# The v phase of a two-block network in wide groups, six of its turns as seven block products

## The chip, the cores and the metric

The kernel runs on one core of a Trainium2 chip. Its time is the device time of one execution in microseconds; lower is better. The time before is the median of three executions.

## The reference

Two blocks run one after the other on x of 256 tokens by 2048 features, all in float32. What touches the change is the first projection of the first block:

```python
h = rmsnorm(x, a_norm)                     # (256, 2048)
z = h @ a_w_in                             # (2048, 3 * 4096): [u | v | gate]
u, v, gate = jnp.split(z, 3, axis=-1)
u = jax.nn.gelu(u)
v = rmsnorm(jax.nn.gelu(v), v_gain)        # over all 4096 columns
sv = einsum('gpq,bnqgc->bnpgc', w_s, v in 8 groups of 512 columns) + b_s
x = x + (u * sv * silu(gate)) @ a_w_out
```

The second block (attention, an mLSTM, a feed-forward layer of 5632 with a convolution) follows. Its last product, `(silu(u_gate) * u_val) @ w_down`, is the "down" phase below.

## The kernel before

**Precision.** Each float32 product is made of three: both operands are split into a high part, the value rounded to the matmul's input type, and a low part, the rest. TensorE adds high by high, high by low and low by high. A matmul has 128 rows of depth, 128 tokens (t = 0 or 1) and 512 columns.

**Chunks and the ring.** Weights come from HBM as a stream of chunks of 256 rows by 512 columns, two blocks of depth side by side (128 x 1024 elements, 512 KB). Four slots hold a chunk and its two parts. SP issues the load when the low part of the chunk four before is made (`load_chunk`, L357). ScalarE makes the high part (`high_of_chunk`, L764) when the load has landed and TensorE is done with the chunk four before; VectorE makes the low part (`low_of_chunk`, L1090); TensorE then multiplies: 12 matmuls per chunk in the v phase (`tokens`, L409), for two blocks of depth, two token tiles and three parts. Each engine runs its own queue in the order in which the code issues it: in the loop of a phase, step n issues `split`, the part of chunk n + 4, and after it whatever else the engine has to do at that step.

**The v phase** is the first: 64 chunks, eight groups of eight. A group gives 512 columns of v for both token tiles in one pair of PSUM banks (`G[0]` or `G[1]`). After a group ScalarE reads the banks with Gelu into `v_all` (`v_out`, L820, its instructions have L779), which also sets the banks free (`group_read`). After the last group the sum of squares of v is taken over all 4096 columns in one piece per token tile, tile 0 on ScalarE (L846) and tile 1 on VectorE (L1192). x itself arrives in five loads; ScalarE and VectorE split it (`in_high`, `in_low`) between the first chunks. The norm's scale for x comes from squares of a second copy, `x_first`, on ScalarE (L834). Before the first operand is there, TensorE runs products of a tile of ones (L457), `WARM_UP` of them.

**The down phase** is the last. It works in wide groups: 1024 output columns, so that four chunks (two rows of chunks by two column halves) form a 2 x 2 block matrix of 256 x 512 blocks, one "turn". A turn of the plain kind is those four chunks (C0, C1 of half 0, C2, C3 of half 1), 48 matmuls. In three turns per group the 2 x 2 block product is made with seven products instead (Strassen's scheme in Winograd's form), of six matmuls each. Each of the seven takes one block, or a sum of blocks, of the weights (128 x 1024 elements again, and again split into high and low), and one block, or a sum, of the activations. The sums of weight blocks are made in place by VectorE (`block_sums`, L1094), four per turn. The sums of activations are made once (`sums_of_rows`, L1541 to L1547) and then split. Products 2, 4 and 3 add straight into banks of the result; 1, 5, 6 and 7 gather in four banks of their own (`XS`), which VectorE combines at the end of a group (`add_products`). A turn by products is mixed with a plain turn's four chunks: the order of its 11 items is `MIXED = (1, "C0", 5, 7, "C1", 6, 3, "C2", 4, 2, "C3")`. `blocks` hold the four weight blocks; SP loads them ahead of items 1, 7 and 4, when the last use of the same block in the turn before is over, in one queue with the chunks.

## Time and profile before

| | us |
|---|---|
| median of three executions | 2125.35 |
| lowest, highest | 2124.49, 2126.13 |
| profiled execution | 2127.12 |
| its span, first to last instruction | 2125.3 |
| TensorE busy | 2116.2 |
| VectorE busy | 1313.1 |
| ScalarE busy | 1045.8 |

The profile records one execution. Matmuls overlap (one that is shown with 390 ns starts 227 ns after the one before), so TensorE's busy share says that it always had something under way, not that it ran at its peak. PE stands for TensorE's matmuls, PEld for its weight loads, DVE for VectorE, ACT for ScalarE, SP for SyncE, which here only issues loads.

### The profile page before, as it was taken

The numbers are of one execution on the slowest core, as the hardware profiler recorded it, in microseconds if no ns is written. First come the engines' busy times: TensorE is split into PE (matmuls) and PEld (weight loads), VectorE is DVE, ScalarE is ACT, GpSimd is POOL, SyncE is SP. The second block draws the span as 40 slices with busy tenths as digits, with TensorE's granted clock in tenths as the row PEclk, the third lists the DMA queues.
The fourth block names the chain that finished last, engine by engine and source line by source line (L and its number), as shares of the span: only waits on it lengthen the run. The fifth ranks groups of instructions, "written<-read, shape, count | busy, mean of one in ns | idle before, by whom it ended". The sixth has DMA issues, their size and how long they took to land.

```text
span 2125.3 us, 24874 instructions
## 1 busy us (share of the span) xinstructions
PE 2116.2 (100%) x10090; PEld 1771.0 (83%) x10090; DVE 1313.1 (62%) x1466; ACT 1045.8 (49%) x1220; POOL 16.6 (1%) x17
## 2 busy tenths in 40 slices
PE   9999999999999999999999999999999999999999
PEld 7888888888888887888888888888888888887887
DVE  5445566656555554554654555567777777779984
ACT  6445444444444444554454444455555555555552
POOL 0000000000000000100000000000000000000000
PEclk9999999999999999999999999999999999999999
DMA  8665566555755555544455565556556556554554
GB/s 303 197 195 172 189 203 204 191 193 179 253 188 188 188 197 170 177 150 149 149 187 190 187 196 186 185 176 189 188 182 195 192 183 194 182 189 178 219 219 157
DMA packets 111810, 404.37 MB, mean 190 GB/s; under 512 B 12496, under 2 KB 13264, under 8 KB 111312
## 3 DMA queue, kind: packets, MB, share of 16 engines
q1 hardware_dynamic: 109440, 394.66, 56.3%
q10 hardware_dynamic: 2256, 8.14, 1.0%
q8 instruction: 79, 1.29, 0.3%
q14 instruction: 35, 0.29, 0.0%
HBM read 400.65 MB, written 2.10 MB: 189 GB/s over the span
## 4 chain that ended last, share of the span: by engine, by line
PE 94%; DVE 4%; DMA 1%; ACT 1%; issue 0%; SPq 0%; ACTq 0%; DVEq 0%
PE g L409 61%; PE xs L428 8%; PE g L428 8%; PE g L693 5%; PE xs L432 4%; PE g L432 4%; DVE w_lo L1090 2%; PE xs L452 1%; DMA raw<-in_stream 1%; PE xs L714 1%; DVE block L1094 1%; PE xs L573 1%; PE g L714 1%; PE xs L481 1%; ACT w_hi L764 0%
## 5 line engine op out<-in xcount | busy, mean ns | idle before, releaser
L1090 DVE TENSOR_TENSOR w_lo<-raw,w_hi 128x1024 fp32r<-128x1024 f32 x719 | 877.5, 1224 | 758.7 <-ACT w_hi L764 755.2
L764 ACT ACTIVATE w_hi<-raw 128x1024 fp32r<-128x1024 f32 x719 | 760.9, 1059 | 956.2 <-PE g L409 643.5
L409 PE MATMUL g<-w_hi,in_both 128*128 128x512 f32 x1536 | 478.5, 391 | 3.3 <-DVE w_lo L1160 3.3
L409 PE MATMUL g<-w_hi,mid_both 128*128 128x512 f32 x1280 | 406.5, 393 | 0.0
L409 PEld LDWEIGHTS g<-w_hi,in_both 128*128 128x128 f32 x1536 | 289.7, 189 | 63.7 <-DVE in_both L1153 3.5
L409 PE MATMUL g<-w_lo,in_both 128*128 128x512 f32 x768 | 299.8, 390 | 0.0
L409 PEld LDWEIGHTS g<-w_hi,mid_both 128*128 128x128 f32 x1280 | 240.4, 188 | 49.6
L409 PE MATMUL g<-w_lo,mid_both 128*128 128x512 f32 x640 | 249.2, 389 | 0.0
L428 PE MATMUL g<-mlp_both,w_hi 128*128 128x512 f32 x704 | 176.7, 393 | 0.4 <-DVE xw L1449 0.4
L428 PE MATMUL xs<-mlp_both,w_hi 128*128 128x512 f32 x704 | 176.3, 392 | 0.0
L409 PEld LDWEIGHTS g<-w_lo,in_both 128*128 128x128 f32 x768 | 144.9, 189 | 29.7
L428 PEld LDWEIGHTS g<-mlp_both,w_hi 128*128 128x128 f32 x704 | 126.6, 189 | 23.5 <-DVE xw L1449 0.8
L428 PEld LDWEIGHTS xs<-mlp_both,w_hi 128*128 128x128 f32 x704 | 126.6, 189 | 22.6
L409 PEld LDWEIGHTS g<-w_lo,mid_both 128*128 128x128 f32 x640 | 120.3, 188 | 23.9
L432 PEld LDWEIGHTS xs<-mlp_both,w_lo 128*128 128x128 f32 x704 | 96.0, 190 | 6.9
L432 PEld LDWEIGHTS g<-mlp_both,w_lo 128*128 128x128 f32 x704 | 96.0, 190 | 6.9
L409 PE MATMUL g<-w_hi,y_hi 128*128 128x512 f32 x256 | 100.0, 390 | 0.0
L693 PE MATMUL g<-w_hi,f_hi 128*128 128x512 f32 x256 | 99.8, 390 | 0.1
L409 PE MATMUL g<-w_hi,y_lo 128*128 128x512 f32 x256 | 99.6, 389 | 0.0
L693 PE MATMUL g<-w_lo,f_hi 128*128 128x512 f32 x256 | 99.6, 389 | 0.0
L693 PE MATMUL g<-w_hi,f_lo 128*128 128x512 f32 x256 | 99.6, 389 | 0.0
L409 PE MATMUL g<-w_lo,y_hi 128*128 128x512 f32 x256 | 99.6, 389 | 0.0
(263 smaller groups left out, 2049.8 us busy)
## 6 DMA issues: line engine op xcount, KB each, us to landing
raw<-in_stream SPq DMA_DIRECT2D x719, 512.0 KB, 3.5
block<-in_stream SPq DMA_DIRECT2D x24, 512.0 KB, 5.4
x_first<-in_x_tokens ACTq DMA_DIRECT2D x1, 2048.0 KB, 9.8
gain_row<-in_gain_rows SPq DMA_DIRECT2D x8, 256.0 KB, 2.7
xt<-in_x_tokens ACTq DMA_DIRECT2D x1, 2048.0 KB, 8.3
xf<-in_x SPq DMA_DIRECT2D x3, 512.0 KB, 9.3
out<-xw ACTq DMA_DIRECT2D x3, 512.0 KB, 3.1
final_row<-in_final_rows ACTq DMA_DIRECT2D x1, 1024.0 KB, 13.3
```

The lines of the kernel that those rows point to most:

```text
L409: ins = mm(G[buf][:, t, :], a[:, kt, at_t], w[:, slot, j * COLS:(j + 1) * COLS], start=(kt == 0 and n == 0), stop=(last and j == ROWS_PER_ ...
L428: mm(UP[buf][:, b, :, :], w_hi[:, slot, j * COLS + b * P:j * COLS + (b + 1) * P], a_both[:, :, kt, :], start=(kt == 0), stop=False, skip_g ...
L432: ins = mm(UP[buf][:, b, 0, :], w_lo[:, slot, j * COLS + b * P:j * COLS + (b + 1) * P], a_both[:, 0, kt, :], start=False, stop=(last and j ...
L452: ins = turn(TR[:, b, t * P:(t + 1) * P], of[:, t, b * P:(b + 1) * P], ident[:])
L481: ins = mm(SV[:, t, :], w[:, t, :], a[:, t, :], start=(n == 0), stop=(n == 2))
L573: ins = mm(to, q[:, t * P:(t + 1) * P], k[:, 0:w], start=n >= HEADS, stop=True, skip_group_check=True)
L693: ins = mm(GG[:, bank, :], a[:, kt, t * P:(t + 1) * P], w[:, slot, half_chunk(j)], start=opens(g, bank), stop=(row == 21 and j == 1 and a ...
L714: ins = mm(bank, a, w[:, slot, half_chunk(j)], start=opens(g, name), stop=(name < 0 and s == BY_PRODUCTS - 1 and j == 1 and n == 2), skip_ ...
L764: activation(w_hi[:, n % RING, :], of[:], ACT.Copy).then_inc(hi_ready, 1)
L1090: v.tensor_tensor(w_lo[:, n % RING, :], of, w_hi[:, n % RING, :].bitcast(F32), ALU.subtract).then_inc(lo_ready, 1)
L1094: v.tensor_tensor(blocks[to][:], blocks[a][:], blocks[b][:], ALU.subtract).then_inc(sem["block_sums"], 1)
```

## The change

The code that described the down phase alone (`DOWN`, `SUMS_AT`, `BY_PRODUCTS`) becomes a list `ITEMS` over all phases, and the v phase is put into wide groups too: four groups of 1024 columns, each with four turns. In `WIDE_STEPS` a pair (a, None) is a plain turn a; (a, b) is plain turn a mixed with turn b by products. The v phase thus has 82 items (19, 22, 19, 22 by group) in place of 64 chunks: items 0 to 7 are plain, 8 to 18 the first mixed turn. The last step of a v group that is mixed has an order of its own, `MIXED_END`, in which half 0 of the result is done at product 2.

```diff
-WARM_UP = 11
+WARM_UP = 17
+WIDE_STEPS = {
+    "v": (((0, None), (1, None), (2, 3)),
+          ((0, 2), (1, 3)),
+          ((0, None), (1, 3), (2, None)),
+          ((0, 2), (1, 3))),
+    "down": (((3, None), (4, None), (8, None), (9, None), (5, 0), (6, 1), (7, 2), (10, None)),
+             ((3, 0), (4, 1), (5, 2), (6, None), (7, None), (8, None), (9, None), (10, None))),
+}
+SUM_TURNS = {"v": (3, 2), "down": (0, 1, 2)}
+SUMS_AT = {"v": (3, 6), "down": (7, 9, 11)}
 MIXED = (1, "C0", 5, 7, "C1", 6, 3, "C2", 4, 2, "C3")
+MIXED_END = (1, "C0", 5, 7, 6, 3, "C1", 4, 2, "C2", "C3")
...
+            def opens(item, bank):
+                key = (item.phase, item.group, bank)
...
+                    _, _, read = group_of(item.phase, 2 * item.group + bank // 2)
+                    if read > 1:
+                        pe.wait_ge(group_read[bank // 2], read - 1)
```

ScalarE at the start splits x later against the chunks, takes the squares of `x_first` at steps 6 and 7 (before 4 and 5), makes the high part of the sums of rows, copies product 1 out of its bank, and applies Gelu in place on what VectorE has written, with the squares of each 512 columns behind it:

```diff
             high_of_chunk(1)
-            in_high(2, 4, 8)
             high_of_chunk(2)
             high_of_chunk(3)
-            in_high(3, 8, 12)
...
+            in_high(2, 4, 8)
+            def sums_high(phase, n):
+                if n in SUMS_AT[phase]:
+                    i = SUMS_AT[phase].index(n)
+                    act.wait_ge(sem["sums_ready"], sums_ahead(phase) + i + 1)
+                    activation(wide[phase].sums_hi[:, i], wide[phase].sums[:], ACT.Copy).then_inc(sem["sums_hi_ready"], 1)
...
+            def v_out(q):
+                act.wait_ge(group_read[q % 2], q // 2 + 1)
+                at_v = v_all[:, :, col_block(q)]
+                by_token(at_v, at_v, ACT.Gelu_apprx_tanh, scale).then_inc(sem["v_ready"], 1)
+                act.wait_ge(sem["v_ready"], q + 1)
+                for t in range(2):
+                    ins = activation(v_junk[:, t, :], at_v[:, t, :], ACT.Square, accum_out=v_ss[:, t, q:q + 1])
+                ins.then_inc(sem["v_sq_ready"], 1)
+                act.wait_ge(sem["v_sq_ready"], q + 1)
+            for n in range(items_of("v")):
+                split("v", n)
+                if n == 0:
+                    in_high(3, 8, 12)
+                if n == 1:
                     in_high(4, 12, 16)
                     act.dma_start(x_first[:], x_tokens).then_inc(sem["x_first_in"], 16)
...
+                sums_high("v", n)
+                if n in (6, 7):
...
+                first_product("v", n)
+                if n == 14:
                     act.wait_ge(sem["scale_ready"], 1)
+                for q in range(7):
+                    if n == half_end("v", q // 2, q % 2) + 1:
+                        v_out(q)
-            activation(y_hi[:, 0:16, :], v_all[:, 0, :], ACT.Square,
-                       accum_out=v_stat[:, 0:1]).then_inc(sem["v_sq_ready"], 1)
```

The eighth output is made at the first step of the next phase. VectorE combines the products and writes the results (after `split`, which holds the low part and the block sum of item n + 4):

```diff
+            def own_products(n):
+                p1, u_a, u_b, u_d = v_wide.p1, v_wide.u_a, v_wide.u_b, v_wide.u_d
+                for g in range(4):
+                    after = n - product_item("v", g, last_by_products("v", g), 6)
+                    if after == 0:
+                        dve.wait_ge(sem["p1_ready"], g + 1)
+                        dve.wait_ge(mm_done, n + 1)
+                        link(v.tensor_tensor(u_a[:], XS[:, 2, :], p1[:], ALU.add))
+                    if after == 1:
+                        link(v.tensor_tensor(u_b[:], XS[:, 3, :], u_a[:], ALU.add))
+                    if after == 2:
+                        link(v.tensor_tensor(u_a[:], XS[:, 1, :], u_a[:], ALU.add))
+                    if after == 3:
+                        link(v.tensor_tensor(u_d[:], XS[:, 1, :], u_b[:], ALU.add))
+                        dve.sem_inc(sem["own_read"], 1)
+            def v_result(q):
+                half = q % 2
+                dve.wait_ge(mm_done, half_end("v", q // 2, half) + 1)
+                to = v_all[:, :, col_block(q)]
+                by_t = ((v_wide.p1, v_wide.u_b), (v_wide.u_a, v_wide.u_d))[half]
+                for t in range(2):
+                    ins = v.tensor_tensor(to[:, t, :], GG[:, 2 * half + t, :], by_t[t][:], ALU.add)
+                ins.then_inc(group_read[half], 1)
+            for n in range(items_of("v")):
+                split("v", n)
+                if n == 0:
+                    in_low(5, 8, 12)
+                if n == 1:
                     in_low(6, 12, 16)
...
+                sums_of_rows("v", n, norm_in.hi, norm_in.lo)
+                sums_low("v", n)
...
+                own_products(n)
+                for q in range(8):
+                    if n == half_end("v", q // 2, q % 2):
+                        v_result(q)
-            link(v.tensor_tensor_reduce(y_lo[:, 0:16, :].rearrange("p a b -> p (a b)"), v_all[:, 1, :],
...
```

`sums_of_rows` makes a set of sums at step n with n + 1 in `SUMS_AT` (steps 2 and 5 of the v phase) by the same five instructions as in the down phase; `sums_low` follows at steps 3 and 6. SP loads chunks and blocks of both wide phases by the rules that the down phase had (`load_chunk`, `load_blocks`). The chunk and product functions of the down phase become `wide_chunk` and `wide_product`, used by both; a chunk or product that opens a bank waits in `opens` until the bank's last result has been read, which in the v phase VectorE's `v_result` reports and no longer Gelu. The down phase keeps its items and their order.

## Rows read from the trace of the kernel before

**Rows 1.** The page, part 1: busy us, share of the span, instructions.

```profile
PE 2116.2 (100%) x10090; PEld 1771.0 (83%) x10090; DVE 1313.1 (62%) x1466; ACT 1045.8 (49%) x1220; POOL 16.6 (1%) x17
```

**Rows 2.** The page, part 4: shares of the chain that ended last, by engine.

```profile
PE 94%; DVE 4%; DMA 1%; ACT 1%; issue 0%; SPq 0%; ACTq 0%; DVEq 0%
```

**Rows 3.** The waits of TensorE: us in total, times, longest.

```profile
PE xs L714 <- DVE w_lo L1090: 0.8, 3, 0.3
```

**Rows 4.** The chain that ended last, down phase: start us, us, what.

```profile
1963.68 1.36 PE xs L714 x6
...
1966.40 2.72 PE g L693 x12
```

**Rows 5.** Stretches: PE, PEld, DVE, ACT, POOL busy (count), PEclk, DMA, GB/s.

```profile
20.00:186.50 166.50, 166.50 (x736) 137.94 (x735) 77.05 (x70) 78.34 (x82) 1.53 (x1) 1.00 0.64 214
...
1952.97:1973.00 20.03, 19.59 (x85) 15.62 (x84) 17.23 (x15) 11.33 (x12) 0.00 (x0) 1.00 0.47 184
```

**Rows 6.** Instructions of VectorE behind the v phase, in order of time.

```profile
188.06 4.42 DVE L1192 CUSTOM_DVE_ANT_0 y_lo<-v_all 128x4096 fp32r<-128x4096 f32 x1
```

**Rows 7.** Instructions of VectorE, down phase: start us, us, engine, line, what.

```profile
1958.03 1.22 DVE L1090 TENSOR_TENSOR w_lo<-block,w_hi 128x1024 fp32r<-128x1024 f32 x1
1959.17 1.22 DVE L1090 TENSOR_TENSOR w_lo<-raw,w_hi 128x1024 fp32r<-128x1024 f32 x1
1960.30 1.22 DVE L1090 TENSOR_TENSOR w_lo<-block,w_hi 128x1024 fp32r<-128x1024 f32 x1
1961.62 1.23 DVE L1094 TENSOR_TENSOR block<-block,block 128x1024 f32<-128x1024 f32 x1
...
1987.77 0.68 DVE L1555 TENSOR_TENSOR u_a<-xs,p 128x512 f32<-128x512 f32 x1
```

**Rows 8.** Instructions of ScalarE, down phase; in brackets the wait before.

```profile
1952.27 1.06 ACT L764 ACTIVATE w_hi<-raw 128x1024 fp32r<-128x1024 f32 x1 [2.95 <-DMA raw<-in_stream]
...
1966.50 1.06 ACT L764 ACTIVATE w_hi<-raw 128x1024 fp32r<-128x1024 f32 x1 [0.30 <-PE g L714]
```

**Rows 9.** Instructions of VectorE that make the sums of rows, down phase.

```profile
1911.56 1.22 DVE L1541 TENSOR_TENSOR f_turn<-f_hi,f_lo 128x1024 f32<-128x1024 f32 x1
1912.82 0.43 DVE L1544 TENSOR_TENSOR f_sums<-f_turn 128x256 f32<-128x256 f32 x1
```

**Rows 10.** Instructions of ScalarE at 29, 186 and 652 us.

```profile
29.29 1.90 ACT L834 ACTIVATE x_junk<-x_first 128x2048 f32<-128x2048 f32 x1
...
186.66 1.25 ACT L779 ACTIVATE v_all<-g,scale 128x512 f32<-128x512 f32 x2
...
652.62 0.61 ACT L792 ACTIVATE sq_junk<-xt 128x512 f32<-128x512 f32 x1
...
653.23 0.62 ACT L792 ACTIVATE sq_junk<-xt 128x512 f32<-128x512 f32 x1
```

**Rows 11.** Instructions of TensorE and ScalarE at the start of the span.

```profile
1.05 4.14 PE L457 MATMUL xs<-ones 128*128 128x128 f32 x22 [1.05 <-DVE ones L1147]
...
8.50 0.77 PE L409 MATMUL g<-w_hi,in_both 128*128 128x512 f32 x1 [3.31 <-DVE w_lo L1160]
...
16.53 1.06 ACT L764 ACTIVATE w_hi<-raw 128x1024 fp32r<-128x1024 f32 x1 [1.14 <-DMA raw<-in_stream]
```

**Rows 12.** A matmul of a product in the down phase, with its wait.

```profile
1959.31 0.50 PE L714 MATMUL xs<-w_hi,sums_hi 128*128 128x512 f32 x1 [0.29 <-DVE w_lo L1090]
```

**Rows 13.** DMA issues, 1930 to 2070 us: count, KB each, median us to landing.

```profile
block<-in_stream SPq DMA_DIRECT2D x20, 512.0 KB, 5.4
```

**Rows 14.** Busy time by stretch at the start, with the granted clock (PEclk).

```profile
4.00:5.00 1.00, 1.00 (x10) 1.00 (x9) 0.00 (x0) 0.00 (x0) 0.00 (x0) 1.00 0.97 315
...
7.00:8.00 1.00, 0.00 (x0) 0.00 (x0) 0.82 (x2) 1.00 (x4) 0.00 (x0) 0.74 1.07 406
...
8.50:14.10 5.60, 5.60 (x13) 4.43 (x14) 5.13 (x10) 5.60 (x12) 0.00 (x0) 0.50 1.02 412
```

**Rows 15.** DMA issues of the first 60 us.

```profile
x_first<-in_x_tokens ACTq DMA_DIRECT2D x1, 2048.0 KB, 9.8
```

More of the change, by code:

```diff
@@ L105 @@
+FIRST_ITEM["end"] = len(ITEMS)
+ITEM_AT = {item: n for n, item in enumerate(ITEMS)}
+CHUNK_ITEMS = [n for n, item in enumerate(ITEMS) if not item.product]
 CHUNK_COUNT = {n: c for c, n in enumerate(CHUNK_ITEMS)}
+QUADS = [(item.phase, item.group, item.turn) for item in ITEMS if item.product == 1]
 B11, B12, B22, B21 = range(4)
@@ new lines, in opens_own, with wide_chunk @@
+            def opens_own(item):
+                key = (item.phase, item.group, -item.product)
+                new = key not in opened
+                if new:
+                    opened.add(key)
+                    if wide_ahead(item.phase, item.group):
+                        pe.wait_ge(sem["own_read"], wide_ahead(item.phase, item.group))
+                return new
+            def wide_chunk(item, a_hi, a_lo, slot):
+                last = ITEM_AT[item] == FIRST_ITEM["end"] - 1
+                order = [(j, t) for j in range(2) for t in range(2)]
+                if last:
+                    order.sort(key=lambda jt: jt[1])
+                for j, t in order:
+                    kt = 2 * item.row + j
+                    if item.phase == "v" and ITEM_AT[item] == 0 and kt == 1 and t == 0:
+                        pe.wait_ge(sem["in_lo_ready"], 2)
+                        pe.wait_ge(lo_ready, 1)
+                    bank = 2 * item.half + t
+                    ended = half_end(item.phase, item.group, item.half) == ITEM_AT[item] and j == 1
+                    for n, (a, w) in enumerate(((a_hi, w_hi), (a_hi, w_lo), (a_lo, w_hi))):
+                        ins = mm(GG[:, bank, :], a[:, kt, t * P:(t + 1) * P], w[:, slot, half_chunk(j)],
+                                 start=n == 0 and opens(item, bank), stop=ended and n == 2, skip_group_check=True)
+                    if last and t == 0 and j == 1:
+                        ins.then_inc(sem["first_tile_done"], 1)
+                return ins
@@ new lines, in wide_product @@
+            def wide_product(item, a_hi, a_lo, slot):
+                p, i = item.product, sum_slot(item.phase, item.turn)
+                sums = wide[item.phase]
+                own = {1: 0, 5: 1, 6: 2, 7: 3}
+                last = item.turn == last_by_products(item.phase, item.group)
+                for j in range(2):
+                    if p in (1, 2, 4):
+                        kt = 4 * item.turn + j + (0 if p == 1 else 2)
+                        t = 1 if p == 4 else 0
+                        hi, lo = a_hi[:, kt, t * P:(t + 1) * P], a_lo[:, kt, t * P:(t + 1) * P]
+                    else:
+                        of = {5: 0, 6: 1, 7: 2, 3: 3}[p]
+                        hi, lo = sums.sums_hi[:, i, of, j, :], sums.sums_lo[:, i, of, j, :]
+                    for n, (a, w) in enumerate(((hi, w_hi), (hi, w_lo), (lo, w_hi))):
+                        first = n == 0 and j == 0
+                        if p in own:
+                            ins = mm(XS[:, own[p], :], a, w[:, slot, half_chunk(j)],
+                                     start=first and opens_own(item), stop=last and j == 1 and n == 2,
+                                     skip_group_check=True)
+                        else:
+                            ins = mm(GG[:, RESULT_OF[p], :], a, w[:, slot, half_chunk(j)],
+                                     start=first and opens(item, RESULT_OF[p]), stop=False, skip_group_check=True)
+                return ins
@@ L747, in high_of_chunk @@
             def high_of_chunk(n):
[L749 to L752 removed]
+                item = ITEMS[n]
+                if item.product:
+                    b, uses = PRODUCT_OF[item.product], quad_of(item)
+                    of = wide[item.phase].blocks[b]
                     if item.product in (1, 3, 2):
@@ L1050, in _ @@
                         gate_tanh(i)
-            for n in range(len(DOWN)):
+            for n in range(items_of("down")):
                 if n == 0:
@@ L1580, in _ @@
[L1580 to L1586 removed]
+                if n + 1 == SUMS_AT["down"][0]:
+                    dve.wait_ge(mm_done, FIRST_ITEM["down"])
+                sums_of_rows("down", n, f_hi, f_lo)
```

466 lines of the change are left out of this document (229 added, 237 removed).

## The prediction, made before the changed kernel was built or run

> **What bounds the kernel now.** I read the page's busy shares first: TensorE is busy over the whole span and its weight loads fill 83% [rows 1]. The chain of waits says the same, 94% on TensorE lines [rows 2], and the wait table has hardly anything for TensorE after the start: 0.8 us in three waits, all in the down phase [rows 3]. So the time is the number of matmuls times their pace, plus the start. The pace stands in the chain of the down phase: 12 matmuls take 2.72 us and 6 take 1.36, 0.2267 each [rows 4]. In the v phase VectorE works 77 of 166 us [rows 5]; it has room there. In the down phase, where blocks are already multiplied by seven products, it works 17.2 of 20.0 us per turn and TensorE loses 0.4 us [rows 5]. That phase is the model for what the change puts into the v phase.
>
> **What it removes.** Six turns go from 48 matmuls to 42: 36 x 0.2267 = 8.2 us off the bound engine. (The Trainium skill, "TensorE: Matmul & The Clock Gate", section "Back-to-back issue gap", gives 512 columns about 216 ns; by it the saving would be 7.8 us. The trace has 227, and that decides.) The one-piece square and sum of v behind the phase (VectorE 4.4 us [rows 6], ScalarE as long beside it) goes away too, worth nothing: TensorE never waited there.
>
> **What it adds.** A turn by products is 11 items in place of 8, and each item takes one high part on ScalarE (1.06 us) and one low part on VectorE (they start 1.13 to 1.14 apart), plus four block sums (1.2) [rows 7, 8]. The v phase has 82 items in place of 64 and 24 block sums; per group come four operations that combine products (0.7) and two results of two operations (1.2 each), priced by the same operation in the down phase [rows 7]; two sets of row sums (1.26 + 4 x 0.4, in all 2.75 with their waits, and 1.2 for their low part, as for any of that size) [rows 9]; and on ScalarE two squares behind each Gelu. A Gelu pair is 1.25 [rows 10]; a square pair, priced by the squares of 512 columns (two start 0.61 apart [rows 10]), 1.3: with the waits of each on the one before, 2.65 for an output that took 1.25. Gelu from SBUF has no row; between 1.2 and 1.3 (the nearest rows) it decides nothing. VectorE then has 82 x 1.14 + 24 x 1.2 + 16 x 0.7 + 8 x 1.2 + 2 x 3.95, and 7 for splitting x: 158 us, for 732 x 0.2267 = 166 us of matmuls. As a mean that fits. But the ring holds four items, so VectorE can't use slack more than four items away, and it needs 2.4 us from the end of an item to the end of the low part in its slot (item end 1966.40, high part 1966.50, about 1.1 to the low part, 1.22) [rows 4, 8]. What decides is each place where products stand close. I went through the queues in the order of the new loops with the durations above; all times below are from the start of the span.
>
> *First products (items 8 to 13), 5.7 us lost.* TensorE starts at 8.65 as before and reaches item 8 at 33.0 and item 11 (product 7) at 38.6. VectorE takes the low part of item 6 at 22.2 (ScalarE splits x until 20.4 and hands over item 6 at 22.2; before, item 4 was at 16.5 [rows 11]), then row sums to 26.1, two low parts and the sums' low part to 29.7, sum, low, sum to 33.2, row sums again to 36.0. ScalarE's next instruction is the high part of those row sums: 36.1 to 37.0. Behind it in its queue stands a square of x_first, 1.9 us [rows 10], then the high part of item 11 at 39.0; its low part ends at 41.3: TensorE waits 2.8. The second square does the same to item 12 (1.6), and the fourth block sum, which comes ahead of the low part of item 13, costs 1.0, small waits 0.3.
>
> *Seam of group 0 to group 1, 5.8 us.* From product 3 of group 0 (46.8) to the first chunk of group 1 TensorE needs 13.6 us, to 60.4. VectorE has in that time seven low parts (8.0), two sums (2.4), four combinations (2.8), the result of half 0 (1.2) and 0.8 of scalars: from 47.0 to 62.1. The chunk opens the bank that the result reads, so it waits: 1.6. Then ScalarE's Gelu and squares of that half (62.1 to 64.8) stand ahead of the high part of product 7: 1.0. Result 1 delays the next low part: 1.0; its Gelu and squares (68.4 to 71.1) delay product 6: 1.2, and the sum behind it product 3: 1.0.
>
> *Seam of group 2 to group 3, 2.3 us*: the same, without the bank and the first of the waits, since two plain turns lie near. *Group 2's first chunk of half 1*, 0.6: it waits for result 3.
>
> *The last turn of groups 1 and 3, 1.4 us each.* It comes behind another turn by products, and has 7, 6, 3 in a row. In the down phase, in the order 7, C1, 6, 3, low parts started at 1958.03, 1959.17, 1960.30, and TensorE waited 0.29 for the first [rows 7, 12]. With C1 moved back, low(6) takes its place and ends at 1960.4, in time; the sum then ends at 1961.8 and low(3) at 1963.0; product 6 has ended at 1962.0: about 1 us, and 0.4 for 7 itself.
>
> Sum: 5.7 + 5.8 + 2.3 + 0.6 + 2.8 = 17.2 us lost, 8.2 saved: +9.0 us. The profiled execution has 2125.3 of span and took 2127.12, 1.8 over the median of 2125.35; on the median the forecast is 2134.
>
> Bounds of the 17.2: from below, the loss that the down phase shows, 0.4 per turn [rows 5], is 2.4 for six. If VectorE were always busy from item 8 on, its work through group 1 (63 us from 28.5, to 91.7) would just meet TensorE (91.5), so the mean alone loses nothing. From above, the loads: blocks landed after 5.4 us in the median where I used 3.5 to 4.5 [rows 13], and one high part waited 2.95 for its chunk [rows 8], which over three seams adds 3 to 4. I take 17 because the waits come from order in queues, which the loops fix.
>
> **The warming.** Before, warming ran from 1.05 to 5.19, then 3.3 us idle [rows 11]. The granted clock was full until about 7.5 (0.74 in that microsecond), and 1.2 GHz for the 13 matmuls from 8.5 to 14.1 [rows 14]. Six more products are 12 passes at 0.1 (ten between 4 and 5 us [rows 14]) to 0.19 (the mean of the 22 before [rows 11]): warming ends at 6.4 to 7.5, before the first operand at 8.5, so it delays nothing. If the clock then stays at 2.4 GHz, 13 x (0.427 - 0.227) = 2.6 us are won, before item 8. But item 11 can't start before 41.3, a time set by ScalarE and VectorE, whatever TensorE did before: I count 0, between 0 and -2.6. (The same page of the Trainium skill, section "HAM oscillation — how this bites in real kernels", has the clock fall back after idle gaps between bursts, so by it a shorter gap may hold the clock, which is rival A's second time. That the clock fell here in the idle stretch agrees.) The order of x and chunks: the first four chunks need only four of the 16 slices of x, so slices 4 to 7 may come later. Nothing waited there, 0. The down phase keeps its items and order: 0. Its third item now waits for VectorE's reading of the last up group, over at about 1895 and needed about 1897.
>
> **Rivals.**
> A, faster: VectorE keeps up. For it: in the down phase the loss is 0.4 per turn although VectorE is 86% busy [rows 5]. Against: there no Gelu, square or result stands between two turns by products, and plain chunks follow. With 2.4 lost: 2125.35 - 8.2 + 2.4 = 2119.6; with the clock held as well 2117.
> B, about the same: the queues are as I say, but the start costs less (squares of x_first or row sums hidden) and ScalarE's Gelu pairs slip into its idle time (in the down phase it idles 8.7 of 20 us per turn [rows 5]). Without the start's 5.7 and half of the first seam: 8.6 lost, 2125.8.
> C, slower still: the loads. SP waits for the last use of block 11 and holds every later chunk behind it; x_first (2 MB, 9.8 us [rows 15]) shares the first loads. With 4 more: 2138. It decides once blocks land later than about 4.5 us after their trigger.
> D: the warming does not hold the clock. Changes A alone, by 2.6.
>
> **How the numbers follow.** Forecast (4.3 to 12 us slower) 0.50, C 0.10, B 0.21, A 0.19. Of this kernel 0.2% is 4.3 us, about what a measurement can tell from no change. Slower by more: 0.60; within: 0.21; faster by more: 0.19. The range leaves out the ends of A and C: 2118 to 2140. The likeliest case's own range is 2130 to 2138.
>
> **What would show it.** TensorE busy in 20 to 195 us should have about 17 us of gaps where before it had none; the wait table should name the low part (w_lo) for TensorE, and results (v_all) at one or two openings; v phase end near 195 in place of 186.6 (its last Gelu starts at 186.66 [rows 10]); VectorE over 90% busy in groups 0, 1 and 3, ScalarE waiting for v results and for sums of rows. Wrong if TensorE's gaps in the v phase sum to under 4 us, or if the ug phase or the down phase moves by itself. The warming is right if the granted clock is full at 8.5.

## The result, and the profile after

| | before | after |
|---|---|---|
| median (lowest to highest), us | 2125.19 (2124.49 to 2126.13) | 2140.19 (2138.62 to 2141.81) |
| profiled execution, its span | 2127.12, 2125.3 | 2141.81, 2140.0 |

The ratio is 1.0070, interval 1.0053 to 1.0088: slower by 15.0 us where 9 were forecast. 2140.19 lies just outside the range given.

The page of the kernel after, part 1, beside [rows 1]: TensorE's share goes from 100% to 99%, VectorE works 71 us more.

```profile
PE 2116.8 (99%) x10066; PEld 1763.2 (82%) x10066; DVE 1383.8 (65%) x1551; ACT 1075.5 (50%) x1274; POOL 16.6 (1%) x17
```

The waits of TensorE after (us in total, times, longest), beside [rows 3]. L605 and L609 are products, L582 chunks. In the v phase nearly all wait for a low part of weights, two openings for VectorE's result; the `u_sum` line is in the down phase, and did not stand there before.

```profile
PE xs L605 <- DVE w_lo L1227: 7.0, 9, 2.1
PE g L609 <- DVE w_lo L1227: 3.7, 5, 0.8
PE g L582 <- DVE w_lo L1227: 3.3, 6, 0.9
PE g L582 <- DVE v_all L1352: 2.5, 2, 2.0
...
PE g L582 <- DVE u_sum L1659: 1.0, 1, 1.0
```

The stretches after (columns as in [rows 5]). In 8.5 to 14.1 the granted clock is full, where it was 0.50 [rows 14]. In 20 to 78 us VectorE is busy 50.1 of 58, and TensorE idles 10.7.

```profile
8.50:14.10 5.60, 5.45 (x24) 4.22 (x23) 3.23 (x4) 2.73 (x3) 0.00 (x0) 1.00 1.03 416
...
20.00:33.00 13.00, 11.95 (x51) 8.85 (x49) 12.76 (x18) 7.22 (x11) 0.00 (x0) 1.00 1.02 415
33.00:50.00 17.00, 12.39 (x39) 8.26 (x39) 14.64 (x19) 11.80 (x14) 0.31 (x1) 0.80 0.19 68
50.00:78.00 28.00, 23.00 (x97) 17.41 (x96) 22.68 (x26) 18.03 (x25) 1.22 (x1) 1.00 0.39 150
78.00:105.00 27.00, 25.56 (x110) 20.16 (x110) 23.35 (x22) 14.47 (x16) 0.00 (x0) 1.00 0.55 205
```

Single matmuls of TensorE after, in order of time. I read each gap as the start of such a row less the end of what came before at 0.2267 us a matmul; in most rows it is some 0.15 more than the wait in brackets.

```profile
7.51 0.47 PE L582 MATMUL g<-w_hi,in_both 128*128 128x512 f32 x1 [0.64 <-DVE w_lo L1295]
...
38.63 0.58 PE L605 MATMUL xs<-w_hi,v_sums_hi 128*128 128x512 f32 x1 [2.10 <-DVE w_lo L1227]
42.68 0.80 PE L605 MATMUL xs<-w_hi,v_sums_hi 128*128 128x512 f32 x1 [1.34 <-DVE w_lo L1227]
47.98 0.50 PE L609 MATMUL g<-w_hi,v_sums_hi 128*128 128x512 f32 x1 [0.71 <-DVE w_lo L1227]
64.02 0.47 PE L582 MATMUL g<-w_hi,in_both 128*128 128x512 f32 x1 [1.96 <-DVE v_all L1352]
...
1908.56 0.47 PE L582 MATMUL g<-w_hi,f_hi 128*128 128x512 f32 x1 [0.98 <-DVE u_sum L1659]
```

| place | forecast, us | gaps measured, us |
|---|---|---|
| first products, items 6 to 13 | 5.7 | 6.6 (1.1, 0.6, 2.3, 1.7, 0.9) |
| seam of groups 0 and 1 | 5.8 | 5.8 (2.1, 0.8, 0.8, 1.1, 1.0) |
| last turn of group 1 | 1.4 | 1.9 (0.6, 0.5, 0.8) |
| group 2's first chunk of half 1 | 0.6 | 0.7 |
| seam of groups 2 and 3 | 2.3 | 2.1 (1.1, 1.0) |
| last turn of group 3 | 1.4 | 2.0 (0.7, 0.5, 0.8) |
| sum in the v phase | 17.2 | 19.1 |
| opening of the down phase | 0 | 1.1 |

By counting matmuls the v phase closes: 732 x 0.2267 = 165.9 from the start at 7.51, 19.1 of gaps, 12 matmuls at 0.427 in place of 0.227 (2.4), and 2.1 at 19 restarts (the matmul behind a wait is followed after 0.31 to 0.34, not 0.227), in all 197.0; the phase's last matmul ends its turn at 199.0, before at 185.4. The 2 us between are three pauses of 0.15 to 0.31 with their restarts (1.1) and a mean pitch of 0.2278 in place of 0.2267 elsewhere (0.7). The phase is 13.6 longer; the first spatial product (the product with w_s, in the next phase), 96 matmuls later, started at 207.19 before and starts at 220.78. The down phase's opening adds 1.1: 14.7, the difference of the spans.

These are the gaps of one execution. In the profile of the changed kernel run again (below) the first products lose 7.9, the seam of groups 0 and 1 4.6, and the last turn of group 3 0.8, with about the same end (the phase ends at 198.6).

### The profile page after: what moved, and what is told of

It reads as the page before. It is cut to its first block, busy times and chain, and to the rows that moved or that the text cites. A ratio compares the mean times of both kernels' runs of the same rounds, so it can differ in the third digit from the quotient of the medians.

```text
span 2140.0 us, 25048 instructions
## 1 busy us (share of the span) xinstructions
PE 2116.8 (99%) x10066; PEld 1763.2 (82%) x10066; DVE 1383.8 (65%) x1551; ACT 1075.5 (50%) x1274; POOL 16.6 (1%) x17
## 4 chain that ended last, share of the span: by engine, by line
PE 90%; DVE 5%; DMA 2%; ACT 2%; issue 1%; POOL 0%; ACTq 0%; SPq 0%; DVEq 0%; POOLq 0%
PE g L494 53%; PE g L582 9%; PE xs L513 8%; PE g L513 7%; PE xs L517 4%; PE g L517 4%; DVE w_lo L1227 3%; DMA raw<-in_stream 2%; PE xs L605 1%; PE g L609 1%; PE xs L536 1%; ACT w_hi L878 1%; DVE v_block L1232 1%; PE xs L738 1%; PE xs L643 1%
## 5 line engine op out<-in xcount | busy, mean ns | idle before, releaser
L1227 DVE TENSOR_TENSOR w_lo<-raw,w_hi 128x1024 fp32r<-128x1024 f32 x695 | 848.6, 1224 | 683.3 <-ACT w_hi L878 679.2
L878 ACT ACTIVATE w_hi<-raw 128x1024 fp32r<-128x1024 f32 x695 | 735.8, 1059 | 896.1 <-PE g L494 559.3
L494 PE MATMUL g<-w_hi,in_both 128*128 128x512 f32 x1024 | 318.6, 390 | 0.0
L494 PEld LDWEIGHTS g<-w_hi,in_both 128*128 128x128 f32 x1024 | 192.2, 188 | 39.8
L494 PE MATMUL g<-w_lo,in_both 128*128 128x512 f32 x512 | 199.2, 389 | 0.0
L494 PEld LDWEIGHTS g<-w_lo,in_both 128*128 128x128 f32 x512 | 96.1, 188 | 19.7
L582 PE MATMUL g<-w_hi,in_both 128*128 128x512 f32 x320 | 104.3, 394 | 6.5 <-DVE w_lo L1227 3.1
L582 PE MATMUL g<-w_hi,f_hi 128*128 128x512 f32 x256 | 100.0, 390 | 1.2 <-DVE u_sum L1659 1.0
L582 PE MATMUL g<-w_lo,f_hi 128*128 128x512 f32 x256 | 99.7, 389 | 0.0
L582 PE MATMUL g<-w_hi,f_lo 128*128 128x512 f32 x256 | 99.6, 389 | 0.0
```

Source lines behind the costliest of these rows:

```text
L494: ins = mm(G[buf][:, t, :], a[:, kt, at_t], w[:, slot, j * COLS:(j + 1) * COLS], start=(kt == 0 and n == 0), stop=(last and j == ROWS_PER_ ...
L582: ins = mm(GG[:, bank, :], a[:, kt, t * P:(t + 1) * P], w[:, slot, half_chunk(j)], start=n == 0 and opens(item, bank), stop=ended and n == ...
L878: activation(w_hi[:, n % RING, :], of[:], ACT.Copy).then_inc(hi_ready, 1)
L1227: v.tensor_tensor(w_lo[:, n % RING, :], of, w_hi[:, n % RING, :].bitcast(F32), ALU.subtract).then_inc(lo_ready, 1)
```

## The experiments

Each time is compared with the kernel before on the same chip at the same time, since medians of one kernel move by about 1 us from one occasion to another (the changed kernel: 15.0 more than before the first time, 16.3 when run again).

| version | median | before beside it | difference |
|---|---|---|---|
| changed kernel (first, again) | 2140.19, 2141.99 | 2125.19, 2125.65 | +15.0, +16.3 |
| changed, 11 warming products | 2142.33 | 2126.06 | +16.3 |
| before, 17 warming products | 2126.30 | 2126.06 | +0.2 |
| wide groups, all turns plain | 2127.28 | 2126.06 | +1.2 |
| changed, squares of v behind the phase | 2137.46 | 2126.06 | +11.4 |
| changed, opening of down without wait | 2141.14 | 2125.70 | +15.4 |
| changed, short squares of x_first | 2139.46 | 2125.70 | +13.8 |
| changed, group 0 plain (five turns) | 2136.15 | 2125.70 | +10.5 |
| changed, blocks loaded once | 2135.53 | 2125.65 | +9.9 |
| changed, filler in the first waits | 2141.16 | 2124.90 | +16.3 |
| filler, squares behind, no down wait | 2135.01 | 2124.90 | +10.1 |
| four turns, sums at 9 and 12 | 2126.83 | 2125.65 | +1.2 |
| four turns, sums at 9 and 31 | 2124.02 | 2124.90 | -0.9 |
| three turns | 2121.65 | 2125.70 | -4.1 |
| three turns, squares behind | 2122.40 | 2125.65 | -3.2 |

Where the row says nothing else, the changed versions keep the 17 warming products; those with three and four turns also leave out the wait at the opening of the down phase, and those with four turns have the squares behind the phase.

The changed kernel once more, as a reference:

> The changed kernel itself once more, beside the next three, as their reference. Both theories: 2140.2, within 1 us.

**The warming.** Alone in the change, and alone in the kernel before:

```diff
-WARM_UP = 17
+WARM_UP = 11
```

> The changed kernel with 11 warming products in place of 17, all else kept. Theory (the start of the v phase is set by the queues of ScalarE and VectorE up to item 11, so a gain of TensorE before it is waited away again): 2140, within 1 us of the changed kernel's 2140.2; the granted clock is 0.50 in 8.5 to 14.1, the first matmuls take 2.6 us more, and the gaps at items 8 and 11 shrink by as much. Rival (the six more products give what they give wherever they stand): 2142.8.

> The kernel before with 17 warming products in place of 11, and nothing else. Theory (the granted clock then stays at 1.00 from the first real matmul, as in the changed kernel, and nothing behind it waits for ScalarE or VectorE): 13 matmuls take 0.227 in place of 0.427, 2.6 us less than before, 2122.6. Rival (the operands set the first 14 us anyway): 2125.2, with gaps of TensorE between 8.5 and 14 in place of the slow matmuls.

With 11 the first matmul is at 8.78, 1.3 later, and 8.5 to 14.1 has a granted clock of 0.70 (0.50 was expected); but product 3 of the first turn starts at 48.43, against 47.98 and, in the second profile of the changed kernel, 48.65. What TensorE gains before item 11 it waits away; the count of 0 for the warming holds. Alone in the kernel before (ratio 0.9991 to 1.0009, that is 1.9 us either way) the forecast of 2.6 missed. In its profile the granted clock is full from 8.5, and two gaps (0.54 and 0.70) stand where a chunk's low part comes late; the operands were not far behind the slow matmuls. The first spatial product is 2.0 sooner there (205.20 for 207.19), in one of the fastest of eleven executions; that nothing at all is gained is not shown.

**Wide groups without products.**

```diff
-    "v": (((0, None), (1, None), (2, 3)),
...
+    "v": (((0, None), (1, None), (2, None), (3, None)),) * 4,
...
+                    if last_by_products("v", q // 2) is None:
+                        ins = v.tensor_copy(to[:, t, :], GG[:, 2 * half + t, :])
```

> The changed kernel with all 16 turns of the v phase plain: wide groups of 1024 columns, 64 items of 12 matmuls, no block products, no sums; VectorE copies each result out of the banks (where the changed kernel adds the combined products) and Gelu and the squares follow in place, warming 17. Theory (the loss sits only where products stand; layout, copy, Gelu in place and squares cost nothing): no gap of TensorE in the v phase; against 2125.2 before, -1.0 for the earlier first operand, -2.6 for the clock at the start, +1.1 for the opening of the down phase: 2122.7. Rival (Gelu in place with its squares, or the bank that waits for VectorE's copy, costs at each seam): 2128 or more, with gaps at the openings of groups. Rival B of the prediction's kind (the wide order alone loses the start): 2130.

The expected 2122.7 missed (ratio 1.0007, 0.9998 to 1.0016), but the 15 us are not here: the profiled v phase has two gaps over 0.31, 1.05 at 11.3 (start) and 0.87 at 59.2 (bank opening), and the first spatial product is 1.0 sooner than before (206.14). What is lost is in the down phase, 235.6 from its first to its last matmul for 233.5 before: the 1.1 of its opening, and five smaller gaps.

**The squares of v.** In one piece behind the phase, as before:

```diff
-                act.wait_ge(sem["v_ready"], q + 1)
-                for t in range(2):
-                    ins = activation(v_junk[:, t, :], at_v[:, t, :], ACT.Square, accum_out=v_ss[:, t, q:q + 1])
-                ins.then_inc(sem["v_sq_ready"], 1)
-                act.wait_ge(sem["v_sq_ready"], q + 1)
...
+                        act.wait_ge(sem["v_ready"], 8)
+                        activation(y_hi[:, 0:16, :], v_all[:, 0, :], ACT.Square,
+                                   accum_out=v_stat[:, 0:1]).then_inc(sem["v_sq_ready"], 1)
...
```

> The changed kernel with the squares of v taken in one piece behind the phase (ScalarE token tile 0, VectorE token tile 1, as in the kernel before) and none behind each Gelu. Theory (at a seam the two squares stand in ScalarE's queue ahead of a high part and make the product wait): the gaps of 0.8 to 1.2 us at the second and third stall of the seams of group 0 to 1 and 2 to 3 go, the wait for the bank and the start stay: about 5 to 6.5 us less, 2134 to 2135. Rival (VectorE alone sets the seams, ScalarE's squares lie beside it): 2139 to 2140.

+11.4 against +15.0 and +16.3: 3.6 to 4.9 us, less than the 5 to 6.5 expected. The gaps of 0.8, 0.8 and 1.1 in 68 to 76 and those of 1.1 and 1.0 in 163 to 167 are gone; the wait for the bank (2.07 at 64.1) and product 3's (0.7) stay. A new gap of 1.2 stands behind the phase, at 209.1. So the squares, from ScalarE's queue, do set these waits of the seams, and not the wait for the bank.

**The opening of the down phase.**

```diff
-                    if read > 1:
+                    if read > 1 and not (item.phase == "down" and item.group == 0 and bank == 2):
```

> The changed kernel, but the down phase's first chunk of half 1 (its third item) no longer waits until VectorE has read the last group of the up phase; the banks it opens were read long before. Theory (the changed kernel's third item waits 0.98 us for VectorE at 1908.56, which the kernel before did not): that wait is gone and nothing is late in its place, the stretch from the first matmul of the down phase to the last is 233.5 as before in place of 234.6, 1.1 us off. Rival (VectorE is late with the next low part anyway, the wait moves to the fourth item): no change.

The wait shrinks from 0.98 at 1908.56 to 0.20 at 1907.84 (bank 3, which the same item opens and I left to wait, took over); no gain could be read from the median. The profiled stretch from the first to the last matmul of the down phase is 234.2, against 234.6 after and 233.5 before, and has a gap of 0.47 at 2061 of the kind that other runs show there too.

**The squares of x_first** (what is left out stands in the expectation):

```diff
-                    activation(x_junk[:, t, :], x_first[:, t, :], ACT.Square,
+                    activation(x_junk[:, t, 0:256], x_first[:, t, 0:256], ACT.Square,
```

> The changed kernel with the two squares of x_first on ScalarE taken over 256 of 2048 columns only (left out: the rest of the sum of squares, so the scale of x is another). Theory (ScalarE's queue: each square of 1.9 us stands ahead of a high part of items 11 and 12): the gap before product 7 (1.74) goes, the one before product 5 (2.26) stays, since the high part of the sums and the low parts of VectorE set it; TensorE idles less after the drop of the granted clock near 39. In all 2 to 4 us less than the changed kernel. Rival 1 (VectorE, with row sums, low parts and block sums, sets the whole start): no change. Rival 2 (the clock falls only because TensorE stands still twice in 10 us): the granted clock stays 1.00 in 39 to 46 and 3 us more are won, 5 to 7 in all.

The first theory missed in its detail: product 7 still starts at 42.26 (42.68 after). Nearly all that goes is behind it: product 6 starts at 43.75 for 45.52, and the bank opens 2.1 us sooner:

```profile
61.90 0.47 PE L582 MATMUL g<-w_hi,in_both 128*128 128x512 f32 x1 [1.39 <-DVE v_all L1352]
```

The clock falls all the same, to 0.50 in 44 to 47. By the medians 1.2 to 2.6 us are gone.

**Group 0 plain.**

```diff
-    "v": (((0, None), (1, None), (2, 3)),
+    "v": (((0, None), (1, None), (2, None), (3, None)),
...
-SUMS_AT = {"v": (3, 6), "down": (7, 9, 11)}
+SUMS_AT = {"v": (6, 9), "down": (7, 9, 11)}
...
```

> The changed kernel with group 0 of the v phase plain (four plain turns) and the sums of rows made later (steps 6 and 9); groups 1, 2 and 3 as they are, so five turns by products in place of six. Theory (products among the first items meet the squares of x_first, the row sums and the splitting of x, and the idle time there lets the granted clock fall): against the changed kernel 1.4 us more for the six matmuls, the gaps of the start (6.6) and of the clock in 39 to 46 (3.0) gone, the seam at group 1 smaller by a part of its 5.8: the v phase 9 to 12 us shorter, 2129 to 2131. The clock granted in 33 to 50 is 1.00. Rival (VectorE's total work decides, and what is taken from the start comes back at the first seam): 2136 or more, with longer gaps in 58 to 80.

2136.15 is the rival's number: 4.6 to 5.9 us less, not 9 to 12. The start's gaps move to two of 1.1, at 39.6 (ScalarE has a high part of row sums and a square of x_first ahead of the high part needed) and at 46.4 (VectorE has the second set of row sums, 42.3 to 45.2, ahead of the low part), among plain chunks; and around the first seam stand 1.1 at 57.3, where the bank opens, 2.1 at 63.6, before product 5, and 0.8, 1.1 and 1.0 behind it, 6.1 in all for the 5.8 after. The granted clock stays at 1.00 here.

**Blocks loaded once.**

```diff
+                if q and item.phase == QUADS[q - 1][0]:
+                    return
                 for b in LOADED_BEFORE.get(item.product, ()):
...
```

The waits for a block count its first load alone.

> The changed kernel with the four weight blocks of a phase loaded once, for its first turn by products, and not for the later ones (left out: 20 of 24 block loads of the v phase and 20 of 24 of the down phase; later products use what the block buffers still hold). Theory (the seams are set by the order of ScalarE's and VectorE's queues, blocks land in time): the gaps of the seams stay, at most 2 us less than the changed kernel run beside it. Rival (the loads: SP holds every chunk behind a block that waits for its last use, and the memory is shared): 4 to 8 us less, the gaps of the seams and of the last turns halved.

6.5 us less than the changed kernel beside it, so the theory's "at most 2" is refuted, and the rival is right in one half. The seams stay within 0.04 (2.08 at 64.2; 0.8, 0.8, 1.1, 1.0 in 69 to 78; 1.1, 1.0 at 162 and 164). The gaps of the last turns of groups 1 and 3, 1.9 and 2.0, are all gone. ScalarE's rows say why. After, just ahead of group 1's last turn:

```profile
83.38 1.06 ACT L878 ACTIVATE w_hi<-v_block 128x1024 fp32r<-128x1024 f32 x1 [2.79 <-DMA v_block<-in_stream]
87.06 1.06 ACT L878 ACTIVATE w_hi<-raw 128x1024 fp32r<-128x1024 f32 x1 [2.62 <-DMA raw<-in_stream]
```

The blocks of the v phase landed 6.7 us after their issue in the median:

```profile
v_block<-in_stream SPq DMA_DIRECT2D x24, 512.0 KB, 6.7
```

With the blocks loaded once ScalarE waits there for TensorE:

```profile
82.46 1.06 ACT L880 ACTIVATE w_hi<-v_block 128x1024 fp32r<-128x1024 f32 x1 [1.67 <-PE g L584]
83.82 1.06 ACT L880 ACTIVATE w_hi<-raw 128x1024 fp32r<-128x1024 f32 x1 [0.30 <-PE g L611]
```

The down phase gains as well (232.2 from its first to its last matmul, 234.9 in the changed kernel beside it, without one gap past its opening). The first spatial product is 4.1 sooner than there (216.28 for 220.36). So by these two profiles some 4 of the 6.5 us belong to the v phase and 2.7 to the down phase.

**The clock.** After the gap at 36.4 to 38.6 the granted clock falls, and 12 matmuls run at 1.2 GHz (0.427 us each for 0.227). The stretch 39 to 45 of the kernel after:

```profile
39.00:45.00 6.00, 4.66 (x12) 3.15 (x10) 3.95 (x4) 6.00 (x7) 0.00 (x0) 0.50 0.27 87
```

I took them, then counted as 3 us and by the rows 2.4, for a cost of their own. The test keeps the waits and keeps TensorE busy in two of them:

```diff
+                if item.group == 0 and item.product in (5, 7):
+                    for _ in range(9):
+                        mm(XS[:, 2, 0:P], ones[:], ones[:], start=True, stop=True)
```

> The changed kernel with nine products of the tile of ones (18 matmuls of 128 columns, as in the warming) put ahead of products 5 and 7 of the first turn by products, where TensorE stands still 2.3 and 1.7 us; they write a bank that product 6 opens later. The waits stay as they are. Theory (the idle time near 36 to 43 lets the granted clock fall to 0.50 for some 6 us, and that costs 3.0 us on top of the gaps): the granted clock is 1.00 from 33 to 55, 3 us less than the changed kernel's 2141 to 2142. Rival (the low parts set these items, a faster TensorE only waits longer): within 1 us of the changed kernel.

The fillers lie in the gaps, and the granted clock is full:

```profile
36.35 2.17 PE L617 MATMUL xs<-ones 128*128 128x128 f32 x18
40.05 2.17 PE L617 MATMUL xs<-ones 128*128 128x128 f32 x18
...
47.93 0.49 PE L609 MATMUL g<-w_hi,v_sums_hi 128*128 128x512 f32 x1 [0.81 <-DVE w_lo L1230]
...
63.96 0.47 PE L582 MATMUL g<-w_hi,in_both 128*128 128x512 f32 x1 [1.91 <-DVE v_all L1355]
```

```profile
33.00:50.00 17.00, 14.14 (x74) 11.19 (x75) 14.64 (x19) 11.80 (x14) 0.37 (x1) 1.00 0.18 66
```

The time is the changed kernel's. Product 3 starts at 47.93 (47.98 after), group 1 opens at 63.96 (64.02): at full clock a new gap of 1.3 stands before product 6. The rival holds, and the slow matmuls cost nothing here. The other profiles say the same: from the first matmul of product 5 to the bank's opening it is 25.39 us in the changed kernel (38.63 to 64.02, slow from 38.9), 25.39 when run again (39.03 to 64.42, slow from 44.5 to 51.3), 25.40 with the filler (38.56 to 63.96, never slow) and 25.39 with 11 warming products (39.07 to 64.46). In the second of these TensorE came late to the bank, and the wait there shrank from 2.1 to 0.9.

The Trainium skill, "TensorE: Matmul & The Clock Gate", section "HAM oscillation — how this bites in real kernels", counts every throttled stretch behind a wait as half lost. The rows agree that the pace halves; here the loss is none, since another engine sets the end of the stretch.

**The three together:** filler, squares behind, no wait at the down phase's opening.

> The changed kernel with all six turns by products and three things at once: the nine filler products ahead of products 5 and 7 of the first turn, the squares of v behind the phase, and no wait of the down phase's third item. Theory (the three add up: 3.0 for the clock, 3 to 4.5 for the squares, 1 for the opening): 2132 to 2134.5, still slower than the kernel before, since the start's and the first seam's waits and the loads of the last turns stay. Rival (they overlap, a wait taken away comes back at the next place): 2136 or more.

+10.1, 6.2 less than the filler alone beside it, what the squares (3.6 to 4.9) and the opening (1) would give together, and nothing of the clock. 2135.01 lies between the theory and its rival. By its profile the clock falls elsewhere, behind the bank's 2.1 us gap (0.94 in 50 to 78).

**Fewer turns, with plain ones around.**

```diff
-    "v": (((0, None), (1, None), (2, 3)),
-          ((0, 2), (1, 3)),
+    "v": (((0, None), (1, None), (2, None), (3, None)),
           ((0, None), (1, 3), (2, None)),
-          ((0, 2), (1, 3))),
+          ((0, None), (1, 3), (2, None)),
+          ((0, None), (1, 3), (2, None))),
...
-SUM_TURNS = {"v": (3, 2), "down": (0, 1, 2)}
-
-SUMS_AT = {"v": (3, 6), "down": (7, 9, 11)}
+SUM_TURNS = {"v": (3,), "down": (0, 1, 2)}
+
+SUMS_AT = {"v": (9,), "down": (7, 9, 11)}
...
-                    if read > 1:
+                    if read > 1 and not (item.phase == "down" and item.group == 0 and bank == 2):
...
```

> A version of three turns by products in place of six: group 0 plain, groups 1, 2 and 3 each plain turn 0, plain turn 1 mixed with turn 3 by products, plain turn 2; one set of row sums, at step 9; 17 warming products; the down phase's third item does not wait. Theory (VectorE and ScalarE have slack as long as a plain turn stands on either side of a turn by products, and no combination or result falls into one): no gap over 0.9 us in the v phase, one at the first seam as in the all-plain version; 18 matmuls less, 4.1 us off the kernel before: 2121 to 2123. Rival (products cost their own waits wherever they stand, some 2 us a turn): 2126 or more.

2121.65, ratio to before 0.9982, 0.9974 to 0.9991: this beats both kernels. Three turns save 18 x 0.2267 = 4.1 us, and 4.1 are measured. That these agree to a tenth is partly luck: the interval goes from 1.9 to 5.5, and by the profile the first spatial product is 5.5 sooner than before (201.72 for 207.19), since the start at full clock counts too. VectorE works 121 of 158 us in 20 to 178.5, no product waits, and the one gap over 0.3 of the v phase is the bank's (second row below).

```profile
20.00:178.50 158.50, 157.42 (x693) 129.59 (x692) 120.70 (x126) 97.94 (x121) 1.53 (x1) 1.00 0.62 222
```

```profile
58.80 0.47 PE L585 MATMUL g<-w_hi,in_both 128*128 128x512 f32 x1 [0.96 <-DVE v_all L1358]
```

> The version with three turns by products, with the squares of v taken in one piece behind the phase as in the kernel before. Theory (its one gap, 1.12 us at 57.7, is result 1, which VectorE makes only after a low part that waits for ScalarE, where Gelu, its table and two squares stand ahead): 1.3 us less on ScalarE there, the gap goes, 0 to 1 us less than that version's 2121.65. Rival (what stands behind the phase then delays the next phase's first chunks): the same or 1 us more, with a wait at the start of the next phase.

The gap at 57.7 goes and one of 0.6 comes at 196, at the start of the next phase. The rival is right: -3.2 and -4.1 can't be told apart.

Four turns, the pair of group 2 side by side:

> As the version with three turns by products and the squares of v behind the phase, but group 2 has two turns by products next to each other, in the changed kernel's order (the second set of row sums at step 12): four turns, 24 matmuls less than before. Theory (each further turn gives 1.36 us, and a pair without a plain turn between costs the waits of its last turn, some 2 us at 90 to 98 in the changed kernel): 0 to 1 us more than with three turns. Rival (only ScalarE's squares made the pair expensive): 1.4 us less than with three turns, 2119.5 to 2120.5.

> The version with four turns by products, the second set of row sums made at step 31 (among group 1's last plain chunks) in place of step 12. Theory (its 2.0 us gap at 52.4, where VectorE makes result 1 late behind these sums, goes, and with it the fall of the granted clock to 0.50 at 55.8 to 59): 4 to 5 us less than its 2126.8, so 2121.5 to 2123, about the version with three turns; the gaps of 0.4 to 0.8 at 120 to 129 stay. Rival (the sums only move the wait to where they are now): 2125 or more.

The first is 4 to 5 us worse than three turns, more than either theory gave. The second set of row sums makes the bank wait, and behind this one gap the granted clock is 0.50 for three microseconds; its eleven runs spread from 2122.4 to 2127.4. TensorE has no idle time in these three microseconds and starts 8 matmuls where 13 fit at full clock, so here the slow clock costs about 1 us (an estimate by that count). With the sums at step 31 that gap is gone and the clock stays up, as expected, but the time is 2.1 less (each against the kernel before beside it) and not 4 to 5: two smaller gaps come where the sums now are (0.4 at 96, 0.7 at 107), and the pair's own (0.9, 0.5, 0.8 at 118 to 127) stay. 2.2 us for a fourth turn that saves 1.4: it costs more than it gives. In the version with the sums at 12:

```profile
54.40 0.47 PE L585 MATMUL g<-w_hi,in_both 128*128 128x512 f32 x1 [1.85 <-DVE v_all L1356]
```

```profile
56.00:59.00 3.00, 3.00 (x8) 2.32 (x7) 1.06 (x1) 2.00 (x4) 0.00 (x0) 0.50 1.01 355
```

## Why the prediction was right in kind and wrong in size

**Right.** The bound engine saves 36 matmuls, and gaps take the saving and more. The mechanism of the seams was as told (Gelu and squares ahead of a high part, the result ahead of a low part): taking the squares away took the gaps that were laid to them away. In the changed kernel the warming gives 0, as counted.

That the table's numbers lie so close is partly luck. The seam of groups 0 and 1 has its 5.8 in one profile and 4.6 in the other. In the first products the forecast let TensorE start at 8.65 with 13 slow matmuls; it started at 7.51 at full clock, 3.7 us ahead, and waited that away. So the gaps stand elsewhere: 2.8, 1.6 and 1.0 were forecast before items 11, 12 and 13, and there are 1.1 before item 7, 0.6 before 9, 2.3 before 10, 1.7 before 11 and 0.9 before 13. The largest, before product 5 (item 10), has the second row sums ahead of the low part in VectorE's queue:

```profile
34.50 1.22 DVE L1314 TENSOR_TENSOR v_rows<-in_both 128x1024 f32<-128x1024 f32 x1
...
37.35 1.22 DVE L1227 TENSOR_TENSOR w_lo<-v_block,w_hi 128x1024 fp32r<-128x1024 f32 x1
```

One sign did not come: VectorE was to be over 90% busy in groups 0, 1 and 3. In 20 to 33 it is (98%), then 86, 81 and 86% in the stretches to 50, 78 and 105, and 83% in group 3: at the seams it stands still itself while ScalarE has Gelu and squares ahead of the high part.

**Wrong: the size of the sum, +9.0 for a measured 14.7 in the spans.** Set against the forecast's own clock, the 5.7 us come in three places.

*1.9 by the opening of group 1* (forecast 62.1, measured 64.02). The step "VectorE takes the low part of item 6 at 22.2" was off: VectorE's rows after have four splits of x before it, and it starts at 23.39.

```profile
20.68 1.22 DVE L1227 TENSOR_TENSOR w_lo<-raw,w_hi 128x1024 fp32r<-128x1024 f32 x1
21.81 1.67 DVE L1288 SCALAR_TENSOR_TENSOR in_both<-xf,par,in_both 128x256 fp32r<-128x256 f32 x4
23.39 1.22 DVE L1227 TENSOR_TENSOR w_lo<-raw,w_hi 128x1024 fp32r<-128x1024 f32 x1
24.53 1.22 DVE L1314 TENSOR_TENSOR v_rows<-in_both 128x1024 f32<-128x1024 f32 x1
```

Each set of row sums takes 2.9, where the sum has 2.75 (its own terms, 1.26 + 4 x 0.4, make 2.86). Nothing gives that back: VectorE has no pause until 41 us, the second row sums end at 37.4 (36.0 in the forecast), item 11 starts at 42.7 (41.3). Behind product 3 VectorE's terms add up to 15.2, to 62.2 and not 62.1, and it has to wait 0.59 for the scale of x, which the sum did not have:

```profile
51.26 0.17 DVE L1375 TENSOR_SCALAR scale_half<-n_rstd 128x2 f32<-128x2 f32 x1 [0.59 <-POOL n_rstd L1777]
```

That this chain, and not TensorE, sets 64.0 is shown by the 25.39 to 25.40 us from product 5 to the opening, in four profiles with different work and clock of TensorE.

*2.7 from there to the end of the phase.* 1.1 of it are the last turns of groups 1 and 3, 1.9 and 2.0 for 1.4 each (in the second profile they are 2.1 and 0.8, so this size is not firm). The step was wrong in kind too: I priced them by the order of block sums and low parts on VectorE, with "blocks landed after 5.4 us in the median where I used 3.5 to 4.5" only as a bound. They landed after 6.7, and with the blocks loaded once no gap is left there: these gaps hang on the loads, rival C's mechanism. The order of the queues has a share too, since with the squares of v behind the phase group 1's last turn keeps only 0.8 of its 1.9. (Whether by the time to landing alone or by the chunks that wait in the queue behind the blocks is not divided.) The seams behind the bank's wait came 0.6 cheaper than forecast (3.7 and 2.1 for 4.2 and 2.3, less 0.1 the other way at the chunk of half 1). Restarts were not in the sum: 13 gaps at 0.11 are 1.4. The rest, 0.8, is in steps too small to list.

*1.1 at the down phase.* "Over at about 1895 and needed about 1897" was wrong in its second half, and the trace of the kernel before shows it. The third item's first matmul, which has to wait now, starts at 1893.84 there, and VectorE reads the up phase's last group until 1894.83:

```profile
1893.84 0.39 PE L693 MATMUL g<-w_hi,f_hi 128*128 128x512 f32 x1
...
1893.61 1.22 DVE L1470 TENSOR_TENSOR u_sum<-xs,u_sum 128x1024 f32<-128x1024 f32 x1
```

That is 1.0 of wait, and 0.98 were measured. The run without that wait has it shrink to 0.20; that this is worth 1.1 in the time is not shown by its median.

Rival A (VectorE keeps up as in the down phase) falls: 19 us of gaps where it gave 2.4. Rival B's "ScalarE's Gelu pairs slip into its idle time" falls with the squares' 3.6 to 4.9 us. Rival C gave 2138, nearest in time; it was to act over the seams, where the loads did nothing, and acts in the last turns. Rival D falls: the clock held in 8.5 to 14.1.

Not settled: why the last turns of groups 1 and 3 lose 3.9 us in one profile of the changed kernel, and 2.9 in the other and with the filler, when the bank opens alike. Most of what parts the first spatial products (220.8, 220.4, 219.6) is there.

## What to carry to other kernels

Block products as here save on the bound engine only while the engines that feed it have room within the depth of the ring (here four items), not on average: VectorE at 77 of 166 us before had room for three turns with plain ones around, and not for six. Before a burst of matmuls is packed tighter, follow the feeding engine's queue instruction by instruction from the last point at which it idled; whatever stands in it ahead of an operand (a square, a result, a sum, a split of another input) can be paid once there is no pause. Price the loads there by when they landed in the trace, not by a better case. Work out from the rows when a bank is needed before adding a wait for it. A slow clock behind a gap is a cost only if TensorE sets the end of that stretch: fill the gap and look whether the next milestone moves before counting it.

## What the runs showed of the hardware that was not expected

The granted clock fell behind gaps of 2.0 to 2.6 us, but not always: with group 0 plain a gap of 2.1 at 63.6 left it at 1.00, and so did the bank's 2.1 at 64.0 in the changed kernel, while in the four-turn version a single gap of 2.0 brought it to 0.50. In two executions of the same changed kernel it fell at 38.9 and at 44.5. Full speed came back in the first at 45.7, in the second at 51.3, and the time from product 5 to the opening of group 1 was 25.39 us in both. A matmul behind a wait costs 0.11 us more than its pitch, beside the wait (0.31 to 0.34 for 0.227): 19 restarts are 2.1 us, more than one turn's saving of 1.36.
